# Context rows of V in four column groups on TensorE, and fetches placed at the instructions that free their rows

## The reference

```
def layer(x, mod, P, rope, k_ext, v_ext):
    h = rmsnorm(x, P['norm_mix_g']) * (1.0 + sc_m) + sh_m
    proj = h @ P['w_in']
    ...
    mixed = concat([attention(q, k, v), hyena(...), chunk_gmlp(...)]) @ P['w_out']
    x = x + g_m * mixed
    h = rmsnorm(x, P['norm_ffn_g']) * (1.0 + sc_f) + sh_f
    return x + g_f * peer(h, ...)

def peer(h, wq, keys, u_tab, v_tab):          # 8 heads, 16 experts of 16384 each
    idx, gate = top 16 of the key scores, softmax of them      # per token and head
    a = gelu(sum_d h[t, d] * u_tab[idx[t, e], d])              # "dot"
    return sum_e gate[t, e] * a[t, e] * v_tab[idx[t, e], :]    # "add"
```

## Time and profile before

| | |
|---|---|
| median of 2 runs | 4677.2 us (4668.66 to 4685.74) |
| span of the profiled execution | 4627.7 us, 39193 instructions |
| PE busy | 3424.7 us (74%) |
| DVE busy | 2972.4 us (64%) |
| POOL busy | 2880.2 us (62%) |
| ACT busy | 1072.4 us (23%) |
| DMA | 1486.11 MB, mean 321 GB/s |
| chain that ended last | DMA 32%, PE 25%, DVE 17%, issue 17%, POOL 6% |

### The profile page before, as it was taken

One profiled execution on the slowest core, in us unless ns is written; L12 is line 12 of the kernel. 1 busy time (PEld: TensorE's weight loads), 2 busy tenths in 40 slices (PEclk: granted clock), 3 DMA queues, 4 the chain that ended last, 5 costly groups with the idle time before them and its releaser, 6 DMA issues.

```text
span 4627.7 us, 39193 instructions
## 1 busy us (share of the span) xinstructions
PE 3424.7 (74%) x9648; PEld 1527.8 (33%) x9648; DVE 2972.4 (64%) x6847; ACT 1072.4 (23%) x2261; POOL 2880.2 (62%) x2564
## 2 busy tenths in 40 slices
PE   8778886678778776677676978946666766667777
PEld 2644653122333332222222546422222222222222
DVE  0279999545566555666664889986666665656662
ACT  1332321121232212121122323211212112121222
POOL 0034555456667676777773545657777777777775
PEclk9889898899999899999998989969999999999999
DMA  7468788989899998999995977879999999999998
GB/s 286 162 224 294 256 298 284 351 314 360 332 354 353 335 370 323 360 376 346 354 377 170 331 257 249 328 258 354 361 355 339 356 360 333 363 341 346 371 370 295
DMA packets 392139, 1486.11 MB, mean 321 GB/s; under 512 B 44108, under 2 KB 45838, under 8 KB 375888
## 3 DMA queue, kind: packets, MB, share of 16 engines
q0 software_dynamic: 368640, 1342.34, 79.5%
q1 hardware_dynamic: 23248, 141.13, 8.0%
HBM read 1480.42 MB, written 2.88 MB: 321 GB/s over the span
## 4 chain that ended last, share of the span: by engine, by line
DMA 32%; PE 25%; DVE 17%; issue 17%; POOL 6%; ACT 3%; POOLq 0%; SPq 0%; DVEq 0%; ACTq 0%
DMA rows_ring<-in_peer_v,idx 19%; DMA rows_ring<-in_peer_u,idx 12%; PE psum L825 12%; POOL rows_ring L548 6%; DVE rows_ring L1366 5%; DVE mix L1380 4%; PE psum L648 4%; PE psum L604 3%; PE psum L770 1%; PE psum L635 1%; DVE small L1288 1%; DMA ring<-in_ada 1%; PE psum L782 1%; PE psum L811 0%; PE psum L597 0%
## 5 line engine op out<-in xcount | busy, mean ns | idle before, releaser
L825 PE MATMUL psum<-rows_ring,diag 128*128 128x512 f32 x4096 | 2067.1, 634 | 901.0 <-DMA rows_ring<-in_peer_v,idx 723.9
L1366 DVE SCALAR_TENSOR_TENSOR rows_ring<-rows_ring,area 128x1024 f32<-128x1024 f32 x1280 | 1562.7, 1225 | 957.9 <-DMA rows_ring<-in_peer_u,idx 935.2
L548 POOL DMA_INDIRECT rows_ring<-in_peer_u,idx x1280 | 1419.7, 1109 | 1084.5 <-DVE rows_ring L1366 431.9
L548 POOL DMA_INDIRECT rows_ring<-in_peer_v,idx x1280 | 1460.3, 1141 | 637.4 <-issue 287.1
L825 PEld LDWEIGHTS psum<-rows_ring,diag 128*128 128x128 f32 x4096 | 730.6, 196 | 2192.0 <-issue 950.6
L1057 ACT ACTIVATE diag<-ident,wts 128x128 f32<-128x128 f32 x1024 | 381.7, 397 | 1515.1 <-PE psum L825 1514.3
L648 PE MATMUL psum<-area,ring 128*128 128x128 f32 (+1 forms) x1344 | 381.8, 443 | 17.1 <-ACT area L919 17.1
L1380 DVE SCALAR_TENSOR_TENSOR mix<-rows_ring,wts,mix 128x1024 f32<-128x1024 f32 x254 | 326.2, 1284 | 8.7 <-DMA rows_ring<-in_peer_v,idx 7.6
L648 PEld LDWEIGHTS psum<-area,ring 128*128 128x128 f32 x1344 | 213.4, 198 | 188.2 <-issue 185.1
L604 PE MATMUL psum<-ring,csil 128*2 128x512 f32 x384 | 176.4, 615 | 21.5 <-DMA ring<-in_ada 21.5
L1049 ACT ACTIVATE acts<-dots 128x16 f32<-128x16 f32 x80 | 17.3, 216 | 555.8 <-DVE rows_ring L1366 555.6
(11 more groups left out here) (174 smaller groups left out, 2473.6 us busy)
## 6 DMA issues: line engine op xcount, KB each, us to landing
ring<-in_ada SPq DMA_DIRECT2D x48, 1024.0 KB, 7.1
ring<-in_win SPq DMA_DIRECT2D x32, 1024.0 KB, 7.7
rows_ring<-in_peer_u,idx POOLq DMA_INDIRECT x1280, 6.1
rows_ring<-in_peer_v,idx POOLq DMA_INDIRECT x1280, 6.2
ring<-in_wout SPq DMA_DIRECT2D x16, 1024.0 KB, 6.7
ring<-in_wq SPq DMA_DIRECT2D x16, 1024.0 KB, 7.3
ring<-in_dft SPq DMA_DIRECT2D x12, 1024.0 KB, 7.7
xT<-in_xT_in SPq DMA_DIRECT2D x1, 2560.0 KB, 15.2
```

The lines of the kernel that those rows point to most:

```text
L548: pool.indirect_dma_start(row(table, k), None, (peer_u, peer_v)[table], bass.IndirectOffsetOnAxis(ap=idx[n][:, k:k + 1], axis=0)).then_inc ...
L825: m = pe.matmul(acc[:, b, :], diag[:, k % 4, :], row(1, k)[:, b * 512:(b + 1) * 512], start=False, stop=False)
L1366: dve.scalar_tensor_tensor(out=row(0, k), in0=row(0, k), scalar=1.0, in1=h_tok[GROUPS[grp][1]][:, bass.ds(t * D_MODEL, D_MODEL)], op0=ALU. ...
```

## The change

1. **Context rows of V.** The additions of context units go from DVE to PE. For this the V rows of a context unit are gathered in another arrangement: in one fetched block lie four experts of 32 tokens. `turn` (PE, 16 small matmuls for a unit) turns indices and weights into this arrangement, `places` (DVE and ACT) copies them out. ACT makes four 128x32 matrices with the weights (`spread`), and PE adds four blocks at once in 8 matmuls: for each half of 512 columns four matmuls, each with 32 columns of weights and 32 partitions of PSUM as its output.
2. **mod.** The 8 matmuls of a mod job go to four column groups in the same way, after one matmul with zeros.
3. **Attention.** The probabilities are only turned (a transpose), not divided. The values of the 8 heads of a tile are laid side by side, divided once by DVE (`an`), and turned by 4 transposes (`ao`). The units run tile by tile, one unit ahead instead of two, in fewer banks of PSUM.
4. **Order.** The loops are gone on all engines. POOL follows ORDER: the job `down` fetches a U row right after the dot that frees its place; the job `up` fetches four V rows right after the addition of the four rows before. Additions come in groups of four rows and lie one and a half units behind the dots instead of one. The close of a tile is three jobs at three places. ROOM has new numbers. The copy of a unit's scores (`stage`) is gone.

```
 def step_jobs(grp, u):
-    for p in range(PIECES):
-        jobs += [("dot", grp, u, p)] if u < n else []
-        jobs += [("add", grp, u - 1, p)] if u else []
-        jobs += [("pick", grp, u + 1, p // 2)] if ...
+    for p in range(QUADS):
+        for i in range(4):
+            k = 4 * p + i
+            if u < n:
+                jobs += [("dot", grp, u, k)]
+                ahead = (u, k + ROWS) if k + ROWS < TOPK else (u + 1, k + ROWS - TOPK)
+                jobs += [("down", grp, *ahead)] if ahead[0] < n else []
+            if i == 0 and context and 0 < u <= n:
+                jobs += [("turn", grp, u - 1, 0)] if p == 0 else [("places", grp, u - 1, 0)] if p == 1 else []
+            if i == 0 and p == 2 and u >= PEER_HEADS + 1 and u % PEER_HEADS == 1:
+                jobs += [("added", grp, u - 2, 0)]
+            if i == 1:
+                if p == 2 and u >= 1 and (u - 1) % PEER_HEADS == 0 and u <= n:
+                    jobs += [("open", grp, u - 1, 0)]
+                m, g = (u - 2, p + 2) if p < 2 else (u - 1, p - 2)
+                if 0 <= m < n:
+                    jobs += [("add", grp, m, g)]
+                m, g = (m, g + 1) if g + 1 < QUADS else (m + 1, 0)
+                if 0 <= m < n:
+                    jobs += [("up", grp, m, g), ("spread", grp, m, g)]
+                if p == 1 and u >= PEER_HEADS + 1 and u % PEER_HEADS == 1:
+                    jobs += [("close", grp, u - 2, 0)]
+            jobs += parts[i - 2:i - 1] if i >= 2 else []
...
-            def fetch(table, grp, u, n, k):
-                pool.wait_ge(s[("u_free", "v_free")[table]], (u + UNIT0[grp]) * TOPK + k + 1)
-                pool.sem_inc(s["pool_tick"], 1)
...
+            for kind, grp, u, p in ORDER:
+                if kind == "down":
+                    fetch_u(grp, u, p)
+                elif kind == "up":
+                    fetch_v(grp, u, p)
...
             def mod(l, st, n, g):
+                    if half == 0:
+                        pe.matmul(g[:, 0:512], zeros[:], w[:, 0:512], start=True, stop=False)
                     for j in range(4):
-                        m = pe.matmul(g[0:2, 0:512], csil[:, 4 * half + j, :], w[:, j * 512:(j + 1) * 512],
+                        m = pe.matmul(g[32 * j:32 * j + 2, 0:512], csil[:, 4 * half + j, :], w[:, j * 512:(j + 1) * 512],
...
             def att_scores(l, st, n):
-                if n >= 3:
-                    pe.wait_ge(s["pt_ready"], done("at", l, st, n - 3))
+                if n >= 2:
+                    pe.wait_ge(s["pt_ready"], done("at", l, st, n - 2))
...
             def att_transpose(l, st, n):
-                    m = pe.matmul(att_bank(st, n)[:, b * P:(b + 1) * P], probs[st][:, n % 2, b * P:(b + 1) * P],
-                                  softmax_diag[:, n % 2, :], start=True, stop=True)
+                    m = pe.transpose(att_bank(st, n)[:, b * P:(b + 1) * P], probs[st][:, n % 2, b * P:(b + 1) * P], ident[:])
...
+            def turn_round(grp, u):
+                v, q = UNIT0[grp] + u, turn_of(grp, u)
+                pe.wait_ge(s["w_ready"], v + 1)
+                for j in range(4):
+                    for a in range(4):
+                        m = pe.matmul(turned[32 * a:32 * a + 32, j, :, :], ident[:, 32 * j:32 * j + 32],
+                                      turn[v % IDX_PLACES][:, :, 4 * a:4 * a + 4], start=True, stop=True)
...
+            def add(grp, u, g):
+                if GROUPS[grp][1] == C_:
+                    pe.wait_ge(s["diag_ready"], 4 * (n + 1))
+                    for j in range(ROWS):
+                        pe.wait_ge(row_landed[1][j], 16 * (n + 1))
                     for b in range(2):
+                        for j in range(ROWS):
+                            m = pe.matmul(psum[32 * j:32 * j + 32, b, :], spread[:, n % 4, j, :], row(1, j)[:, b * 512:(b + 1) * 512],
+                                          start=False, stop=False)
+                    m.then_inc(s["v_free"], 4)
+                else:
+                    for j in range(ROWS):
+                        pe.wait_ge(s["diag_ready"], 4 * n + j + 1)
+                        pe.wait_ge(row_landed[1][j], 16 * (n + 1))
+                        for b in range(2):
+                            m = pe.matmul(acc[:, b, :], diag[:, j, :], row(1, j)[:, b * 512:(b + 1) * 512], start=False, stop=False)
+                        m.then_inc(s["v_free"], 1)
...
-            def att_norm(l, st, n):
-                link(dve.reciprocal(rinv[:, n % 2:n % 2 + 1], rowsum[:, n % 2:n % 2 + 1]))
-                dve.tensor_scalar(softmax_diag[:, n % 2, :], ident[:], rinv[:, n % 2:n % 2 + 1], None, ALU.mult
+            def att_norm(l, st, t):
+                dve.wait_ge(s["pv_mm"], done("av", l, st, 8 * t + 7))
+                link(dve.reciprocal(rinv, rowsum[:, t % 2, :]))
+                dve.tensor_tensor(out_rows.rearrange("p (h d) -> p h d", h=8), out_bank.rearrange("p (h d) -> p h d", h=8),
```

445 lines of the change are left out of this document (211 added, 234 removed).

## The result

The changed kernel takes 4876.4 us (median of two runs, 4876.0 to 4876.8) against 4677.2 us: ratio 1.042, 95% interval 1.039 to 1.046. It is 4% slower, and the forecast of no change (4690 us, range 4540 to 4830) was wrong.

What follows compares the result with a forecast made beforehand. No single bound: POOL nearly full in latent stages, DVE then PE in woven latent mixers, nothing full in the woven context mixer. Terms +80 -25 -35 -10 +24 -35 +14 = +13 us, giving 4690 us, range 4540 to 4830.

Steps and rivals of the forecast that it cites:

- Context additions, +80 us: Two woven latent mixers: additions moved from DVE to PE, 2.05 us a group of four, lengthen each mixer by about 40 us.
- The signs that I named: Right: latent mixers with PE over 93%, DVE under 65%; wrong: latent units of 50 us, clock well under 0.97.
- Modulation, -25 and -35: Mod jobs fall from 7.03 to 2.8 us: 25 us less at the start, 35 less in layer 1's woven context mixer.
- The table, -10: Woven context mixer of layer 1: new costs in ROOM spread the rest of the work better, 10 us less.
- Fetches in fours +24: Latent units: V and U fetches in groups of four hide barely, 0.5 us more a unit over 47 units.
- ends of tiles -35: Six tile ends: POOL's 7.33 us of standing hides but for 1 to 2 us, 35 us less.
- later additions +14: Ends of latent groups: V units begin and end 8 rows later, 7 us more for each latent group.
- Attention, counted inside the mixers as a gain: Attention in the latent mixers: 153 against 161 us, 8 us less a mixer, as waits for the diagonal end.
- The second: Rival: fetches in fours stall in latent units, 4 us more each over 47 units, 188 us, 4854 us; chance 20%.
- The first: Rival: DVE was the real bound in the latent mixers, so relieving it makes the kernel faster, 4516 us; chance 24%.
- The third: Rival: column groups do not overlap, each context addition costs 7.0 us instead of 2.05, 320 us, 5010 us; chance 4%.
- The base: The sum was made against the profiled span, 4627.7 us; 49.5 us were added to reach the runs' median, 4677.2 us.

Runs made afterwards that it cites:

- the control: The kernel before the change, unchanged, run and profiled once more: ratio 1.00 (4685.6 against 4673.5 us).
- e2: The changed kernel with the placement table ROOM of the kernel before, nothing else different: ratio 1.025.
- e12: The changed kernel with only the first four V rows fetched for the context, and with before's ROOM table: ratio 0.985.
- e14: e15 with V's ring for the context at eight rows, two fours in turn, fetched one addition earlier: ratio 1.020.
- e15: The changed kernel with before's ROOM table and two places instead of four in the weight blocks' ring: ratio 1.045.
- e7: e5 with attention undone as well (two units ahead, division by a scaled diagonal): ratio 0.986, 4612.3 us.
- e5: The changed kernel with context additions on DVE again, a row at a time, and before's ROOM table: ratio 1.001.
- e4: The kernel before with one part of the change alone, modulation in four column groups: ratio 0.992.
- e11: e5 with the probabilities turned by ordinary multiplications with the identity instead of transposes: ratio 0.996.

## Why the prediction was wrong, step by step

**Context additions, +80 us: this is the step that failed. The mixers are 224 us longer than in the control.** The price of a group on PE was right at full clock: eight matmuls in 1.92 us (2.05 taken). The mean over both mixers is 2.85 us (182.3 / 64), since many run at half the clock. The trace does not agree with the estimate of 2.3 us by the Trainium skill (TensorE: Matmul & The Clock Gate, Measured speedup vs the span model), which was too high. The 16 turns took 7.7 us together, 0.48 each, less than the 1.6 taken.

What failed is the wait. The sum let an addition wait for its rows only in the last stretch, six times; elsewhere it counted PE's work alone. But the same ring of one four holds in the whole mixer, and its cycle of 14 us is near the 562 / 32 = 17.6 us that an addition had on average, so many slips become a wait: for PE at a landing, for POOL at PE, for DVE at U's rows behind POOL. The fetches, with all that waits on them, cost 89 and 98 us a mixer (e2 against e12), and a second four in the ring gave 76 and 72 back (e14 against e15).

By place: +36 ahead of attention (11 taken), of which the table has 24; +10 in attention (-8 taken); +68 behind it (39 taken). The cycle itself was put at 10.5 us and is 13.7 to 14.9. The addition runs at half the clock (3.64 us), 0.80 us to the first fetch was not counted, and the landing was taken at 4.2 to 4.5 us, near the least of the earlier trace rows, whose median is 6.1: in the last six cycles of each mixer the addition starts 5.6 to 6.7 us after the fourth fetch. The sum also left out the clock in these mixers. Summed over the stretches of the trace with a granted clock of 0.5, PE is busy 137 of its 540 us at that level in this mixer (control: 74 of 467; e12: 78 of 503).

The parts do not simply add. Taken one behind the other from e7 to the changed kernel, the new attention costs 33 and 34 us a mixer (e5), the additions on PE then 59 and 51 (e2), the new table then 24 and 31. The additions cost less on this path than their waits do, because they also have a gain in them: 59 us is the 89 of fetches and waits less the 30 by which e12 is shorter than e5.

**The signs that I named.** PE was to be busy over 93% in these mixers; it was 79 to 80%, with DVE at 50%. That pair, both engines with room, is what a chain through a short ring looks like. Of the signs of being right, the eight matmuls in about 2 us, the first index near 210 us and latent units of 47 us did come. Of those of being wrong, the clock in the latent stages fell well under 0.97, to 0.86, and the last one is no longer for it (1576 against 1583 us).

**Modulation, -25 and -35.** The start came as worked out: 238.3 to 213.5 us in e4. Of the woven -35 the profiles show 10, which is within their noise there. I had let PE's saved time count as the stage's time, though PE was busy 699 of 925 us in it.

**The table, -10: it cost about 55 us** in the two mixers (677.5 and 678.8 against 653.3 and 648.2 us), and gave nothing measurable in the woven stage (1731 and 1728). I had looked at the stage that it was to help and not at the one before it.

**Fetches in fours +24, ends of tiles -35, later additions +14: the sum of +3 was too high.** e7 differs from e4 by these parts and is faster by 0.6% of 4677, 27 us (5 to 48 by the ends of the two intervals). They were not run apart. A unit takes 47.3 us after, 47.4 before and 48.1 in the control (mean of units 2 to 31 of layer 1), so the +24 was not there, though the clock did fall as feared, from 0.97 to 0.86. A unit with a tile's end takes 50.5 instead of 53.7 us in the best case, not 6 us less; at the next tile's end it is 53.3 against 53.2.

**Attention, counted inside the mixers as a gain.** The sum took -8 us a mixer there. In the new form its stretch is 31 and 39 us longer where DVE still adds (e5 against e7). Where PE adds it takes 151 and 149 us, at a clock of 0.80, and without V's fetches 139 and 133 us (e12), against 141 and 142 in the control. So the new form costs time only together with additions on DVE, or with the waits.

**The rivals.** The second had the right sign and nearly the right number (4854), at the wrong place. Its mechanism, POOL standing behind a V fetch that waits for PE, did decide, but in the mixers; the latent stages that it spoke of did not change. The first (DVE was the bound, and its relief makes it faster) was half right: DVE was the bound of the mixers, with 499 of 563 us in the control. But PE is next at 503 of 564 us (e12): even with no fetch to wait for, the relief of DVE leaves the mixers at 564 and 550 us. The third, no overlap, is excluded by 1.92 us for eight matmuls. That the measured 4876 us lies near the second rival's number is luck.

**The base.** I added 49.5 us to come from the profile to the median. The control, whose profile is 56 us longer, shows that 46 of these sit in the two long stages (1705 and 1563 against 1731 and 1583 us). The profile before was a short one, so adding the difference was right; the changed kernel's profile and median differ by 2 us.

## What to carry to other kernels

When work moves to an in-order engine that has other work, count the ring that feeds it: if one place must be fetched, landed and used before the next fetch starts, that cycle against the mean distance of the uses (here 14 against 17.6 us) tells whether there is room, and the price of the operation (1.92 us) does not. A second place gave back 74 us a mixer, of some 94. Price an engine's relief by the next engine's busy share. Of a change in many parts, keep those that pay: modulation in column groups is 0.8% faster alone, and with fetches in fours and the new tile ends 1.4% faster than the kernel before.

## What the runs showed of the hardware

- Less work can take longer. In attention e5 has 581 matmul records and 165 us of busy PE, e7 702 records and 125 us. The mean granted clock was 0.54 and 0.91. The turns are transposes in e5 and multiplications in e7; multiplications in e5's order (e11) give 151 us at 0.71.
- The clock need not matter: in the last latent stage it is 0.96 in the control and 0.86 after and in e7, and that stage is not longer (1583, 1576 and 1561 us).
- Four column groups of 128x32 at once: eight matmuls of 512 columns in 1.92 us at 2.4 GHz and 3.64 us at 1.2 GHz, against 7.03 us for eight without groups at full clock, 3.7 times faster.
- A fetch of 128 rows by index, in the chain: 0.94 us of POOL and 0.30 us to the next, and 5.6 to 6.7 us from the fourth fetch's start to the addition that waited for its rows.
